# Pair sums on VectorE, a shared stationary operand for the gate weights, and a feature-major p, in a kernel of two transformer blocks

## The chip, the core and the metric

The kernel runs on one core of a Trainium2 chip. All inputs are float32 in the chip's main memory. The metric is the device time of one launch in microseconds (us), the median of several runs. TensorE is the engine for matrix products, VectorE (DVE in the profile) and ScalarE (ACT) work element by element, GpSimd (POOL) here mostly issues DMAs and adds a few tables, and SyncE (SP) issues the loads of the weights. Engines run on their own and meet only at semaphores.

## What is computed

256 tokens of width 2048 go through two blocks. Cut to what the change touches:

```
# first block, diff attention: per head (4 heads, width 256)
out = (softmax(q0 k0) - lam * softmax(q1 k1)) @ v
out = out * rsqrt(mean(out*out) + eps) * g * 0.8          # over the 256 features
# ... w_out, feed-forward ...
e = (p @ w_ple_proj) * sigmoid(rmsnorm(h) @ w_ple_gate)   # p: 256 tokens x 256
h = h + rmsnorm(e)

# second block
h = rms_norm(x)
z = h @ w_in                       # 16 of its columns are gates: mlstm input, forget, fox forget
ha = mlstm(q, k, v, gates)         # per head (4 heads, width 256)
ha = rms_norm(ha) * sigmoid(mo)    # over the head's 256 features
# ... fox attention, w_out, feed-forward ...
x = x + sigmoid(rms_norm(x) @ w_ple_gate) * (p_2 @ w_ple_proj)
```

## The kernel before

**Layout.** Activations stand feature-major: a tile is 128 features by 256 tokens, and the width of 2048 is 16 such tiles. Each float32 operand of a large product is held as two parts, hi (rounded) and lo (the rest), side by side in one array, such as `X1[:, kt, 0, :]` and `X1[:, kt, 1, :]`. A product then takes the hi part of the weights against hi and lo of the activations (512 columns, line 1923) and the lo part of the weights against hi alone (256 columns, line 1925), or three products of 512 columns (lines 1933 to 1935).

**The stream of weights.** SyncE loads weights into a ring, two halves of four tiles at a time. For each half `m` ScalarE writes the hi part (`hi`, line 589), DVE the lo part (`lo`, line 1154), and TensorE multiplies (`blocks`). ScalarE and DVE work three halves ahead (`LEAD`). Each engine's program is the same loop over halves, `each_half`: ScalarE and DVE first do the split of the half, then what `after(m)` asks for; TensorE first does what `before(m)` asks for, then the half's products. All order within an engine is this order of the program. An attention head is a group of 16 halves (`MIX`), a branch group also 16.

**The norm over a head.** A head's output of 256 features is two tiles. At the end of its group (m = 15 in diff, 13 in mLSTM, 14 in the first of them) DVE writes it to `MX[:, 0:2]`, ScalarE squares it into `MX[:, 2:4]` (`o_square`, line 690), and both go on with the next group. There, ahead of half 2, TensorE sums the squares over the features by two products with a matrix of ones (`sum_o`, lines 2058 and 2059, each float32 product appears as two records), then ScalarE takes the root (`o_norm`, line 694), DVE the reciprocal (line 1341) and the gains (line 1422 or 1730), ScalarE and DVE split the result into `X2` (lines 698 and 1346). This happens eight times, n = 0 to 7: four diff heads and four mLSTM heads. Diff head 0's sum is taken in the group of head 1, and so on; n = 3 falls into the first branch group, n = 7 into the first group of the fox attention. In the first branch group TensorE waits for `o_ready` ahead of half 4.

**The gates.** In the first mLSTM group, ahead of half 5, TensorE multiplies 16 gate columns of `w_in_2` (`gate_split`, hi and lo) by the activations: per tile one product of 512 columns (line 2223) and one of 256 (line 2224), accumulated over 16 tiles in `pw[0:16, 0]`. Then a chain of small steps counted by the semaphore `gates` follows: ScalarE copies the second half of the columns (line 955), DVE adds it (line 1664), scales and adds the bias (1666, 1668), ScalarE takes abs, exp and ln, DVE combines (1671), and TensorE turns the result ahead of half 7 (line 2231).

**p.** GpSimd loads `p` token-major into `emb[k]`. TensorE transposes it by four small products ahead of half 2 of `out1` (k = 0) and of the second `gate1` group (k = 1) (`embed`, line 2115) into `pw[:, 2]`; ScalarE writes its hi part and DVE the lo part (lines 780 and 1467) into `X2[:, 12:14]`, which the projection multiplies.

Of the kernel before, what the change touches and what calls it, by code (L numbers as in the profile page):

```python
# [170 lines left out]
def two_blocks(nc, a, out):  # L171
# [94 lines left out]
    x_turned, eps_ready, zeros_ready = sem("x_turned"), sem("eps_ready"), sem("zeros_ready")  # L266
    p_turned, p_hi, p_ready = sem("p_turned"), sem("p_hi"), sem("p_ready")
    lam_parts, lam_summed, lam_exps = (sem(n) for n in ("lam_parts", "lam_summed", "lam_exps"))
# [7 lines left out]
    probs_turned, pt_ready, pv_done = sem("probs_turned"), sem("pt_ready"), sem("pv_done")  # L276
    o_raw, o_squares, o_sums, o_root, o_normed, o_hi, o_ready = (sem(n) for n in ("o_raw", "o_squares", "o_sums", "o_root", "o_normed", "o_hi", "o_ready"))
    sig_done, gated, ple_gated, out_ready = (sem(n) for n in ("sig_done", "gated", "ple_gated", "out_ready"))
# [195 lines left out]
    def _(pool):  # L474
# [26 lines left out]
        pool.wait_ge(o_ready, 12)  # L501
        pool.dma_start(emb[0], a["p"][0, 0].rearrange("(a p) d -> p a d", p=P)).then_inc(p_landed, 16)

# [11 lines left out]
        pool.wait_ge(hid_ready, 32)  # L515
        pool.dma_start(emb[1], a["p_2"][0, 0].rearrange("(a p) d -> p a d", p=P)).then_inc(p_landed, 16)
        for j in range(6, 12):
# [56 lines left out]
    def _(act):  # L574
# [202 lines left out]
        def embed(k, operand):  # L777

            act.wait_ge(p_turned, k + 1)
            A(operand[:, :, 0, :], pw[:, 2, :].rearrange("p (a t) -> p a t", a=2), ACT.Copy).then_inc(p_hi, 1)  # L780

# [175 lines left out]
        def gate_steps(m):  # L957

            if m == 0:
                square_h(6, 0)  # L960
                square_h(6, 1)
            if m == 1:
                gained_hi(4, 3, "mix_norm_g_2")
            if m == 2:
                square_h(6, 2)
                square_h(6, 3)
            if m == 3:
                root(6)
            if m == 4:
                row(2, 3, mix_rn)  # L970
            if m == 5:

                act.wait_ge(ple_left, 16 * 4)
                gate_step(2, GR[0:16, 0], pw[0:16, 0, TOK:512], ACT.Copy)
                gate_step(5, GR[0:16, 2], GR[0:16, 1], ACT.Abs)
                gate_step(6, GR[0:16, 2], GR[0:16, 2], ACT.Exp, scale=-1.0)
                gate_step(7, GR[0:16, 2], GR[0:16, 2], ACT.Ln, bias=1.0)
            if m == 6:
                gate_step(10, small[:, 0:32], pw[:, 1, 0:32], ACT.Copy)
            if m == 7:  # L980
                gate_step(12, GR[0:16, 4], pw[0:16, 2, 0:TOK], ACT.Copy)
            if m == 9:
                gate_step(23, GR[0:4, 3], GR[0:4, 2], ACT.Exp, scale=-1.0)
                gate_step(25, small[:, 48:56], pw[:, 0, 0:8], ACT.Copy)
# [157 lines left out]
    def _(dve):  # L1142
# [191 lines left out]
        def o_lo_heads(k, tile):  # L1334
            for hh in range(2):
                dve.wait_ge(o_hi, k + hh + 1)
                TT(X2[:, bass.ds(tile + hh, 1), 1, :], pw[:, 2 + hh, 0:TOK].unsqueeze(1), X2[:, bass.ds(tile + hh, 1), 0, :], ALU.subtract).then_inc(o_ready, 1)

        def o_inverse_root(n):
            dve.wait_ge(o_root, n + 1)  # L1340
            steps.step(nc.vector.reciprocal(rn[:, 1, :], rn[:, 0, :]))
            settled()
# [37 lines left out]
        def diff(i):  # L1380
# [14 lines left out]
            def after(m):  # L1395
                if m == 3:
                    evac_normed(s, 0, QK[:, 0:2, :], mix_rn)
                if m == 7:
                    evac_normed(s, 1, QK[:, 2:4, :], mix_rn)
                    turn_by_angles(s)  # L1400
                if m == 8:
                    swap_halves()
                if m == 9:
                    rope_sum()
                if m == 11:
                    evac_values(s, 2, 0)
                if m == 12:
                    logits(2 * i + 8, 2 * i + 8, mask_tables, SCALE)
                    combine()
                if m == 15:  # L1410
                    dve.wait_ge(pv_done, 8 + i + 1)
                    nc.vector.tensor_copy(MX[:, 0:2, :], pw[:, 2:4, 0:TOK]).then_inc(o_raw, 1)
                    evac_normed(s, 3, t[:, (s.u + 3) % 2], mix_rn)
                if m == 2 and not isinstance(i, int):
                    finish_diff(i - 1)
# [12 lines left out]
        def branch(i):  # L1428
            s = At("branch", i, 8, 6)

            def after(m):
                if isinstance(i, int) and i == 0 and m == 2:
                    finish_diff(3)
# [31 lines left out]
        def embed(k, operand):  # L1465
            dve.wait_ge(p_hi, k + 1)
            TT(operand[:, :, 1, :], pw[:, 2, :].rearrange("p (a t) -> p a t", a=2), operand[:, :, 0, :], ALU.subtract).then_inc(p_ready, 1)

# [185 lines left out]
        def gate_steps(m):  # L1654
# [7 lines left out]
            if m == 5:  # L1662
                dve.wait_ge(gates, 2)
                TT(GR[0:16, 1], pw[0:16, 0, 0:TOK], GR[0:16, 0], ALU.add).then_inc(gates, 1)
                dve.wait_ge(gates, 3)
# [21 lines left out]
        def mlstm(i):  # L1687
            s = At("mlstm", i, 8, 4)
            first = isinstance(i, int)

            def after(m):
                if m == 2 and not first:
                    finish_mlstm(i - 1)
# [44 lines left out]
        def fox(i):  # L1738
# [16 lines left out]
            def after(m):  # L1755
# [14 lines left out]
                if m == 16:  # L1770
                    o_lo_heads(16 + 4 * i, 8 + 4 * i)
                if i == 0 and m == 2:
                    finish_mlstm(3)
# [128 lines left out]
    def _(pe):  # L1902
# [152 lines left out]
        def sum_o(n):  # L2055

            pe.wait_ge(o_squares, n + 1)
            MM(pw[:, 1, 0:TOK], ones, MX[:, 2, :], start=True, stop=False)
            MM(pw[:, 1, 0:TOK], ones, MX[:, 3, :], start=False, stop=True).then_inc(o_sums, 1)

# [48 lines left out]
        loop(pe, Chain(None), 4, 0, lambda i: each_half(At("branch", i, 8, 6), BRANCH), start=1)  # L2109
        def embed(k):  # L2110

            pe.wait_ge(p_landed, 16 * (k + 1))
            for f in range(2):
                for q in range(2):
                    ins = T(pw[:, 2, f * TOK + q * P:f * TOK + q * P + P], emb[k][:, q, f * P:f * P + P], ident)
            ins.then_inc(p_turned, 1)

        def out1(i):
            s = At("out1", i, 8, 2)

            def before(m):
                if i == 0 and m == 2:
                    embed(0)
            each_half(s, OUT1, x1_is(1), before)
        out1(0)
# [77 lines left out]
        each_half(at, GATE, x1_is(3), last_turn, start=4)  # L2203
        each_half(At("gate1", 1, 8, 2), GATE, x1_is(3), lambda m: embed(1) if m == 2 else None)

# [9 lines left out]
        def gate_steps(m):  # L2215
# [3 lines left out]
            if m == 5:  # L2219
                norm_row(2, 3)  # L2220
                pe.wait_ge(gate_split_lo, 1)
                for kt in range(KT):
                    MM(pw[0:16, 0, :], gate_split[:, kt, 0, :], X1[:, kt], start=kt == 0, stop=False, skip_group_check=True)
                    ins = MM(pw[0:16, 0, 0:TOK], gate_split[:, kt, 1, :], X1[:, kt, 0, :], start=False, stop=kt == KT - 1, skip_group_check=True)
                ins.then_inc(gates, 1)
# [164 lines left out]
```

## Time and profile before

| | us |
|---|---|
| median of 3 runs | 2807.81 (2807.31 to 2809.17) |
| the profiled execution, device time | 2807.58 |
| its span, first to last instruction | 2805.8 |
| TensorE busy, of the span | 2768.0 (99%) |
| DVE busy | 1801.6 (64%) |
| ScalarE busy | 1377.4 (49%) |
| mean granted clock of TensorE | 0.998 |

The profile's times count from the first instruction of the one execution that was recorded. "PE" is TensorE's products and "PEld" its weight loads, which run beneath the products. A line such as "x2" merges two neighbouring instructions. A product's record lasts longer than the distance to the next one, since products are pipelined: what a product costs is read from start to start. "Idle before" in square brackets is the time in which the engine waited, and what ended the wait.

### The profile page before, as it was taken

To read this page: it belongs to the slowest core of one execution; us is meant where nothing else is said; L and a number is where in the kernel's file an instruction comes from. 1 tells how busy PE (TensorE), PEld (TensorE's weight loads), DVE (VectorE), ACT (ScalarE), POOL (GpSimd) and SP (SyncE) were. 2 spreads that over 40 slices of the span, in tenths; PEclk is the share of its full clock that TensorE was granted. 3 is DMA by queue.
4 is the path that set the end of the run, shared out by engine and by line. 5 is a ranking of instruction groups with operands and counts; after the bars stand their busy time and mean duration, and the time that the engine had idled before them with its cause. 6 is when DMAs were issued, how large, how long until landed. Compare 5 with 4: busy or idle time off the path is not lost.

```text
span 2805.8 us, 39633 instructions
## 1 busy us (share of the span) xinstructions
PE 2768.0 (99%) x14572; PEld 2358.9 (84%) x14572; DVE 1801.6 (64%) x2112; ACT 1377.4 (49%) x1751; POOL 54.9 (2%) x67
## 2 busy tenths in 40 slices
PE   8999999999999999999999999999999999999999
PEld 6888888888888888888877888878888888888887
DVE  7676766665655656556566666775676567657655
ACT  4555554455544434444466555554544345444453
POOL 2000000000000000000000100000000000000000
PEclk9999999999999999999999999999999999999999
DMA  8555546565566565565655555545555555555654
GB/s 263 178 179 166 177 159 196 191 195 181 181 204 186 194 194 180 195 193 196 195 187 184 196 169 169 158 139 191 181 193 191 192 186 179 199 191 180 232 186 136
DMA packets 413227, 521.98 MB, mean 186 GB/s; under 512 B 8544, under 2 KB 320048, under 8 KB 412496
## 3 DMA queue, kind: packets, MB, share of 16 engines
q1 hardware_dynamic: 410384, 510.64, 55.8%
q0 software_dynamic: 2752, 10.11, 1.3%
q8 instruction: 59, 0.97, 0.1%
q14 instruction: 32, 0.26, 0.0%
HBM read 516.51 MB, written 4.21 MB: 186 GB/s over the span
## 4 chain that ended last, share of the span: by engine, by line
PE 93%; DVE 4%; ACT 2%; issue 1%; DMA 0%; SPq 0%; ACTq 0%; DVEq 0%
PE ps L1923 38%; PE ps L1925 19%; PE ps L1933 11%; PE ps L1935 11%; PE ps L1934 11%; DVE E L1744 1%; DVE split L1154 1%; PE pw L2041 1%; ACT split L589 1%; PE pw L1988 0%; DVE X L1264 0%; PE pw L2042 0%; ACT junk L628 0%; PE pw L2036 0%; DMA raw<-in_w_in 0%
## 5 line engine op out<-in xcount | busy, mean ns | idle before, releaser
L1154 DVE TENSOR_TENSOR split<-raw,split 128x1024 fp32r<-128x1024 f32 x960 | 1157.1, 1226 | 678.3 <-ACT split L589 673.4
L589 ACT ACTIVATE split<-raw 128x1024 fp32r<-128x1024 f32 x960 | 1002.8, 1055 | 823.1 <-PE ps L1935 446.4
L1923 PE MATMUL ps<-X,split 128*128 128x512 f32 x4352 | 1376.5, 398 | 12.6 <-DVE split L1154 8.5
L1925 PEld LDWEIGHTS ps<-X,split 128*128 128x128 f32 x4352 | 818.7, 188 | 193.6
L1925 PE MATMUL ps<-X,split 128*128 128x256 f32 x4352 | 856.2, 278 | 0.0
L1923 PEld LDWEIGHTS ps<-X,split 128*128 128x128 f32 x4352 | 666.1, 189 | 16.4 <-issue 10.2
L1933 PE MATMUL ps<-split,X 128*128 128x512 f32 x1408 | 550.3, 391 | 4.7 <-ACT E L805 1.2
L1935 PE MATMUL ps<-split,X 128*128 128x512 f32 x1408 | 548.1, 389 | 0.0
L1934 PE MATMUL ps<-split,X 128*128 128x512 f32 x1408 | 547.9, 389 | 0.0
L1933 PEld LDWEIGHTS ps<-split,X 128*128 128x128 f32 x1408 | 264.3, 188 | 60.8 <-DVE split L1154 1.9
L1935 PEld LDWEIGHTS ps<-split,X 128*128 128x128 f32 x1408 | 264.3, 188 | 55.0
L1934 PEld LDWEIGHTS ps<-split,X 128*128 128x128 f32 x1408 | 264.4, 188 | 54.2
L595 ACT ACTIVATE cross<-ps 128x512 f32<-128x512 f32 x160 | 95.7, 598 | 256.9 <-PE ps L1925 256.9
L1923 PE MATMUL ps<-split,X 128*128 128x512 f32 x512 | 163.0, 400 | 0.3 <-ACT small L666 0.3
L1925 PEld LDWEIGHTS ps<-split,X 128*128 128x128 f32 x512 | 96.2, 188 | 22.7
L1167 DVE TENSOR_TENSOR t<-ps,cross 128x512 f32<-128x512 f32 x74 | 51.2, 691 | 85.2 <-ACT cross L595 85.2
L1925 PE MATMUL ps<-split,X 128*128 128x256 f32 x512 | 100.6, 278 | 0.0
L1923 PEld LDWEIGHTS ps<-split,X 128*128 128x128 f32 x512 | 78.3, 189 | 2.9 <-issue 2.3
L1167 DVE TENSOR_TENSOR E<-ps,cross 128x512 f32<-128x512 f32 x54 | 37.3, 690 | 48.4 <-ACT cross L595 47.3
L845 ACT ACTIVATE X<-t 128x512 f32 (+1 forms) x32 | 20.2, 632 | 74.9 <-DVE t L1528 74.9
L1530 DVE TENSOR_TENSOR X<-t,X 128x512 f32 (+1 forms) x32 | 22.2, 692 | 32.2 <-ACT X L845 32.2
L1097 ACT ACTIVATE X<-t 128x512 f32 (+1 forms) x22 | 13.9, 631 | 52.4 <-DVE t L1845 52.4
(237 smaller groups left out, 1147.2 us busy)
## 6 DMA issues: line engine op xcount, KB each, us to landing
raw<-in_w_up SPq DMA_DIRECT2D x152, 1024.0 KB, 5.5
raw<-in_w_in SPq DMA_DIRECT2D x134, 1024.0 KB, 5.2
raw<-in_w_down SPq DMA_DIRECT2D x108, 1024.0 KB, 5.2
raw<-in_w_out SPq DMA_DIRECT2D x32, 1024.0 KB, 5.1
raw<-in_w_ple_gate SPq DMA_DIRECT2D x32, 1024.0 KB, 5.2
raw<-in_w_br_moba SPq DMA_DIRECT2D x8, 1024.0 KB, 5.5
raw<-in_w_br_diff SPq DMA_DIRECT2D x8, 1024.0 KB, 5.3
raw<-in_w_ple_proj SPq DMA_DIRECT2D x4, 1024.0 KB, 5.3
```

Source lines behind the costliest of these rows:

```text
L589: A(split[:, k % RING, :, 0, :], raw[:, (k // 2) % RING, HALF * (k % 2):HALF * (k % 2) + HALF, :], ACT.Copy).then_inc(hi_done, 1)
L595: A(cross[:, s], ps[:, 2 * s:2 * s + 2, TOK:512], ACT.Copy).then_inc(cross_done, 1)
L1154: TT(split[:, k % RING, :, 1, :], raw[:, (k // 2) % RING, HALF * (k % 2):HALF * (k % 2) + HALF, :], split[:, k % RING, :, 0, :], ALU.subtr ...
L1167: steps.step(TT(dst, ps[:, 2 * s:2 * s + 2, 0:TOK], cross[:, s], ALU.add))
L1530: TT(X2[:, bass.ds(4 * i + 2 * u, 2), 1, :], tile, X2[:, bass.ds(4 * i + 2 * u, 2), 0, :], ALU.subtract).then_inc(hid_ready, 1)
L1744: steps.step(nc.vector.reciprocal(MX, MX))
L1923: MM(ps[:, 2 * s + j, :], stay[:, 0, j * P:j * P + P], move, start=start, stop=False, skip_group_check=True)
L1925: ins = MM(ps[:, 2 * s + j, 0:TOK], stay[:, 1, j * P:j * P + P], move[:, 0, :], start=False, stop=stop, skip_group_check=True)
L1933: MM(dst, x_hi, w[:, :, 0, :], start=start, stop=False, skip_group_check=True)
L1934: MM(dst, x_hi, w[:, :, 1, :], start=False, stop=False, skip_group_check=True)
L1935: ins = MM(dst, x_lo, w[:, :, 0, :], start=False, stop=stop, skip_group_check=True)
L2041: MM(pw[:, bank, 0:TOK], values(0), pt[:, 0:TOK], start=True, stop=False, skip_group_check=True)
```

## The change

Three edits. First, DVE adds the two tiles of squares into `MX[:, 2]` (`o_pair_sum`) in `after(1)` of the group in which `sum_o` falls, and `sum_o` takes one ones-product, which waits for that addition instead of for the squares. Second, the hi and lo parts of the gate weights, 16 columns each, are one stationary operand of 32 columns: one product of 512 columns per tile, with output in 32 partitions. ScalarE copies all of it, and DVE brings partitions 16 to 31 down with a shuffle and makes two additions instead of one. Third, `p` and `p_2` are stored feature-major before the launch, so GpSimd's loads bring them as they are needed, the transposes go, and ScalarE and DVE split them straight from the loaded array. The diff, cut:

```diff
@@ gpsimd
-        pool.dma_start(emb[0], a["p"][0, 0].rearrange("(a p) d -> p a d", p=P)).then_inc(p_landed, 16)
+        pool.dma_start(emb[0], a["p_t"].rearrange("p (f t) -> p f t", f=2)).then_inc(p_landed, 16)
...
-        pool.dma_start(emb[1], a["p_2"][0, 0].rearrange("(a p) d -> p a d", p=P)).then_inc(p_landed, 16)
+        pool.dma_start(emb[1], a["p_2_t"].rearrange("p (f t) -> p f t", f=2)).then_inc(p_landed, 16)
@@ scalar
         def embed(k, operand):
-            act.wait_ge(p_turned, k + 1)
-            A(operand[:, :, 0, :], pw[:, 2, :].rearrange("p (a t) -> p a t", a=2), ACT.Copy).then_inc(p_hi, 1)
+            act.wait_ge(p_landed, 16 * (k + 1))
+            A(operand[:, :, 0, :], emb[k], ACT.Copy).then_inc(p_hi, 1)
...
-                gate_step(2, GR[0:16, 0], pw[0:16, 0, TOK:512], ACT.Copy)
+                gate_step(2, GR[0:32, 0:2], pw[0:32, 0, :].rearrange("p (a t) -> p a t", a=2), ACT.Copy)
@@ vector
+        def o_pair_sum(n):
+            dve.wait_ge(o_squares, n + 1)
+            TT(MX[:, 2, :], MX[:, 2, :], MX[:, 3, :], ALU.add).then_inc(o_pair_sums, 1)
...
         def diff(i), after(m)
+                if m == 1 and not isinstance(i, int):
+                    o_pair_sum(i - 1)
                 if m == 2 and not isinstance(i, int):
                     finish_diff(i - 1)
...
         def branch(i), after(m)
+                if isinstance(i, int) and i == 0 and m == 1:
+                    o_pair_sum(3)
...
         def embed(k, operand):
             dve.wait_ge(p_hi, k + 1)
-            TT(operand[:, :, 1, :], pw[:, 2, :].rearrange("p (a t) -> p a t", a=2), operand[:, :, 0, :], ALU.subtract).then_inc(p_ready, 1)
+            TT(operand[:, :, 1, :], emb[k], operand[:, :, 0, :], ALU.subtract).then_inc(p_ready, 1)
...
                 dve.wait_ge(gates, 2)
-                TT(GR[0:16, 1], pw[0:16, 0, 0:TOK], GR[0:16, 0], ALU.add).then_inc(gates, 1)
+                steps.step(nc.vector.stream_shuffle(GR[0:32, 2], GR[0:32, 0], HALVES_SWAPPED))
+                steps.step(TT(GR[0:16, 1], GR[0:16, 0], GR[0:16, 1], ALU.add))
+                settled()
+                TT(GR[0:16, 1], GR[0:16, 1], GR[0:16, 2], ALU.add).then_inc(gates, 1)
...
         def mlstm(i), after(m)
+                if m == 1 and not first:
+                    o_pair_sum(i + 3)
...
         def fox(i), after(m)
+                if i == 0 and m == 1:
+                    o_pair_sum(7)
@@ tensor
         def sum_o(n):
-            pe.wait_ge(o_squares, n + 1)
-            MM(pw[:, 1, 0:TOK], ones, MX[:, 2, :], start=True, stop=False)
-            MM(pw[:, 1, 0:TOK], ones, MX[:, 3, :], start=False, stop=True).then_inc(o_sums, 1)
+            pe.wait_ge(o_pair_sums, n + 1)
+            MM(pw[:, 1, 0:TOK], ones, MX[:, 2, :], start=True, stop=True).then_inc(o_sums, 1)
...
-        def embed(k):
-            pe.wait_ge(p_landed, 16 * (k + 1))
-            for f in range(2):
-                for q in range(2):
-                    ins = T(pw[:, 2, f * TOK + q * P:f * TOK + q * P + P], emb[k][:, q, f * P:f * P + P], ident)
-            ins.then_inc(p_turned, 1)
...
                 for kt in range(KT):
-                    MM(pw[0:16, 0, :], gate_split[:, kt, 0, :], X1[:, kt], start=kt == 0, stop=False, skip_group_check=True)
-                    ins = MM(pw[0:16, 0, 0:TOK], gate_split[:, kt, 1, :], X1[:, kt, 0, :], start=False, stop=kt == KT - 1, skip_group_check=True)
+                    ins = MM(pw[0:32, 0, :], gate_split[:, kt].rearrange("p a c -> p (a c)"), X1[:, kt], start=kt == 0, stop=kt == KT - 1)
                 ins.then_inc(gates, 1)
@@ host
+    for name in ("p", "p_2"):
+        arrays[name + "_t"] = np.ascontiguousarray(arrays.pop(name)[0, 0].T.reshape(2, P, TOK).transpose(1, 0, 2)).reshape(P, 2 * TOK)
```

## Rows read from the trace of the kernel before

**Rows 1.** The page, busy time, share of the span and instructions of each engine.
```profile
PE 2768.0 (99%) x14572; PEld 2358.9 (84%) x14572; DVE 1801.6 (64%) x2112; ACT 1377.4 (49%) x1751; POOL 54.9 (2%) x67
```

**Rows 2.** TensorE's waits, whole run: who for whom, total us, times, longest.
```profile
PE ps L1923 <- DVE split L1154: 8.5, 3, 7.9
PE pw L2029 <- DVE E L1747: 4.0, 2, 2.0
...
PE pw L2036 <- DVE E L1393: 1.9, 4, 0.5
```

**Rows 3.** Order of time, 260 to 276: start, us, instruction, [idle before].
```profile
268.28 2.36 DVE L1154 TENSOR_TENSOR split<-raw,split 128x1024 fp32r<-128x1024 f32 x2 [1.99 <-ACT split L589]
...
269.61 0.59 PE L2058 MATMUL pw<-E,con 128*128 128x256 f32 x2
...
270.04 0.59 PE L2059 MATMUL pw<-E,con 128*128 128x256 f32 x2
```

**Rows 4.** Order of time after the second diff head, 311 to 324, and 320.9.
```profile
318.46 3.50 DVE L1154 TENSOR_TENSOR split<-raw,split 128x1024 fp32r<-128x1024 f32 x3 [3.05 <-ACT split L589]
...
318.73 0.59 PE L2058 MATMUL pw<-E,con 128*128 128x256 f32 x2
...
320.74 1.22 DVE L1154 TENSOR_TENSOR split<-raw,split 128x1024 fp32r<-128x1024 f32 x1
```

**Rows 5.** Order of time at the last diff head and the branch after it.
```profile
416.67 3.50 DVE L1154 TENSOR_TENSOR split<-raw,split 128x1024 fp32r<-128x1024 f32 x3 [3.04 <-ACT split L589]
...
416.96 0.59 PE L2058 MATMUL pw<-E,con 128*128 128x256 f32 x2
...
419.85 0.48 ACT L694 ACTIVATE rn<-pw,small 128x256 f32<-128x256 f32 x1
...
423.72 0.69 DVE L1346 TENSOR_TENSOR X<-E,X 128x512 fp32r<-128x512 f32 x1 [0.70 <-ACT X L698]
...
424.47 0.73 PE L1923 MATMUL ps<-X,split 128*128 128x512 f32 x2 [0.91 <-DVE X L1346]
```

**Rows 6.** Order of time after the second mLSTM head, 1627 to 1632.
```profile
1627.92 2.36 DVE L1154 TENSOR_TENSOR split<-raw,split 128x1024 fp32r<-128x1024 f32 x2 [1.65 <-ACT split L589]
...
1629.60 0.59 PE L2058 MATMUL pw<-E,con 128*128 128x256 f32 x2
```

**Rows 7.** Groups by line and shape: total us, mean ns, idle before.
```profile
L1306 DVE STREAM_SHUFFLE E<-E 32x1024 f32<-32x1024 f32 x8 | 10.7, 1343 | 0.0
...
L1717 DVE TENSOR_TENSOR rn<-rn,G 128x256 f32<-128x256 f32 x4 | 1.7, 420 | 1.1 <-ACT rn L1004 1.1
...
L780 ACT ACTIVATE X<-pw 128x512 fp32r<-128x512 f32 x2 | 1.1, 571 | 0.0
```

**Rows 8.** Order of time around the gate weights' matmuls, 1530 to 1548.
```profile
1537.68 0.39 PE L2223 MATMUL pw<-X,gate_split 128*16 128x512 f32 x1
...
1537.91 0.28 PE L2224 MATMUL pw<-X,gate_split 128*16 128x256 f32 x1
...
1538.02 0.63 PE L1923 MATMUL ps<-X,split 128*128 128x512 f32 x2
...
1538.28 0.37 ACT L955 ACTIVATE E<-pw 16x256 f32<-16x256 f32 x1 [4.28 <-PE pw L2224]
...
1543.36 0.40 PE L1925 MATMUL ps<-X,split 128*128 128x256 f32 x2
...
1544.43 0.26 PE L2231 MATMUL pw<-con,E 16*128 16x16 f32 x2 [0.67 <-DVE E L1671]
```

**Rows 9.** Order of time around the first `embed`, 588 to 602.
```profile
597.01 0.39 PE L1935 MATMUL ps<-split,X 128*128 128x512 f32 x1
...
597.91 0.40 PE L1934 MATMUL ps<-split,X 128*128 128x512 f32 x1
```

**Rows 10.** Stretches: length, busy us of each engine, granted clock, DMA share, GB/s.
```profile
24.00:28.00 4.00, 4.00 (x14) 3.41 (x13) 4.00 (x9) 0.04 (x1) 0.00 (x0) 0.50 0.68 236
...
1881.00:1891.00 10.00, 7.99 (x41) 6.76 (x41) 9.04 (x25) 5.75 (x13) 0.00 (x0) 1.00 0.31 106
```

More of the change, by code:

```diff
@@ L266, in two_blocks @@
     x_turned, eps_ready, zeros_ready = sem("x_turned"), sem("eps_ready"), sem("zeros_ready")
-    p_turned, p_hi, p_ready = sem("p_turned"), sem("p_hi"), sem("p_ready")
+    p_hi, p_ready = sem("p_hi"), sem("p_ready")
     lam_parts, lam_summed, lam_exps = (sem(n) for n in ("lam_parts", "lam_summed", "lam_exps"))
@@ L276, in two_blocks @@
     probs_turned, pt_ready, pv_done = sem("probs_turned"), sem("pt_ready"), sem("pv_done")
-    o_raw, o_squares, o_sums, o_root, o_normed, o_hi, o_ready = (sem(n) for n in ("o_raw", "o_squares", "o_sums", "o_root", "o_normed", "o_hi", "o_ready"))
+    o_raw, o_squares, o_pair_sums, o_sums, o_root, o_normed, o_hi, o_ready = (sem(n) for n in ("o_raw", "o_squares", "o_pair_sums", "o_sums", "o_root", "o_normed", "o_hi", "o_ready"))
     sig_done, gated, ple_gated, out_ready = (sem(n) for n in ("sig_done", "gated", "ple_gated", "out_ready"))
@@ L2109, in _ @@
         loop(pe, Chain(None), 4, 0, lambda i: each_half(At("branch", i, 8, 6), BRANCH), start=1)
-        def embed(k):
-            pe.wait_ge(p_landed, 16 * (k + 1))
-            for f in range(2):
-                for q in range(2):
-                    ins = T(pw[:, 2, f * TOK + q * P:f * TOK + q * P + P], emb[k][:, q, f * P:f * P + P], ident)
-            ins.then_inc(p_turned, 1)
-        def out1(i):
[L2119 to L2124, printed above, removed]
+        def out1(i):
+            each_half(At("out1", i, 8, 2), OUT1, x1_is(1))
         out1(0)
@@ L2203, in _ @@
         each_half(at, GATE, x1_is(3), last_turn, start=4)
-        each_half(At("gate1", 1, 8, 2), GATE, x1_is(3), lambda m: embed(1) if m == 2 else None)
+        each_half(At("gate1", 1, 8, 2), GATE, x1_is(3))
         s = At("proj2")
```

## The prediction

> **What bounds the kernel now.** I read the page first: TensorE is busy for 99% of the span [rows 1]. That share alone is modelled, so the second view is what TensorE waited for [rows 2]. The list adds up to 31 us in 2805.8, of which 7.9 is one wait at the start. In the body TensorE runs from matmul to matmul, and the other engines work in its shadow. So whatever is taken off TensorE is gained, and whatever it is made to wait for is lost, almost one for one. The third view is the order of time around each place that the diff touches. There I look for two things: where TensorE stands when it reaches the changed instruction, and where VectorE (DVE) stands at that moment.
>
> **Pair sums: what TensorE saves.** A ones-product of 256 fp32 columns takes 0.43 us: the first starts at 269.61 and the second at 270.04 [rows 3]. Eight calls lose one each: 8 x 0.43 = 3.4 us less.
>
> **Pair sums: the new wait.** TensorE now waits, ahead of half 2 of the next unit group, for an addition that DVE issues in `after(1)`, so behind `lo(0)` and `lo(1)` of that group. Before, it waited for ScalarE's squares, which were long there. The question is where DVE is at that time. It is late: ScalarE squares, waits and takes the sigmoid at the end of the group before, and only then turns to the next halves' splits, so DVE's run of subtractions begins after 3.05 us of idleness, at 318.46. TensorE is at the ones-products at 318.73, when `lo(0)` has hardly begun [rows 4]. The third subtraction of that run starts at 320.74, which is 2.28 us after the first. Nothing holds it back there, so the pair sum takes this very place. Queued behind it on DVE is the third subtraction (half 5's operand), which TensorE needs over 8 us later (a half takes about 2.8 us), so the delay there costs nothing.
> An addition of 128x256 fp32 takes 0.42 us [rows 7]. From DVE's end to TensorE's start I take 0.06 us (423.72 + 0.69 = 424.41, then 424.47) [rows 5]. With S for the start of DVE's first subtraction, the product starts at S + 2.28 + 0.42 + 0.06 = S + 2.76. It takes 0.43, and I add 0.10 for a first matmul after an idle time, an estimate from row 424.47, where two matmuls show 0.73 and not the usual 0.63 [rows 5, 8]. So half 2 begins at S + 3.29. Before it began at T + 0.86 (two products), T being the start of the first. The loss is (S - T) + 2.43.
> - n = 0: S = 268.28, T = 269.61 [rows 3]: 1.10 us. ScalarE loads its table early in this unrolled stretch, so S is earlier.
> - n = 1: 318.46 and 318.73 [rows 4]: 2.16. n = 2 repeats it (S - T = -0.28): 2.15. n = 4, the first mLSTM head's, is the same picture with -0.22: 2.21.
> - n = 5: 1627.92 and 1629.60 [rows 6]: 0.75. n = 6 and 7 repeat it to 0.01: 2.25 for the three.
> - n = 3: 416.67 and 416.96 give 2.14. But here TensorE already lost 1.06 us two halves later, waiting for `o_ready`: it started at 424.47 after 0.91 by the row [rows 5]. Such idle times come out some 0.15 short, since a matmul's record runs past the start of the next (0.67 and 0.83 in rows 8, below), so it was free at 423.41. Now it comes there at 416.67 + 3.29 + 5.6 = 425.56. The chain before `o_ready` starts with a square root at 419.85, whose table is loaded already. The new product ends about 420.2, so the chain moves by 0.35 us, to 424.8, and the wait is gone. The loss at n = 3 is 425.56 - 424.57 = 0.99. If the table load should come behind the wait, it would be 1.6.
> Sum: 1.10 + 2.16 + 2.15 + 0.99 + 2.21 + 2.25 = 10.9 us lost, the saved products already deducted. What follows `sum_o` (square root, reciprocal, gains) starts no later relative to TensorE than before, since TensorE itself was held, so I find no second stall. The handover may be 0.15 instead of 0.06 and the first matmul's 0.10 may be nothing: 10.1 to 11.7, and up to 12.3 with n = 3.
>
> **Gate weights.** Before, each of 16 tiles has a matmul of 512 and one of 256 columns, starting 0.23 and 0.11 to 0.12 us apart [rows 8]. Sixteen times 0.115 is 1.8 us less. The weight loads, 32 instead of 16 columns, lie beneath the 512-column matmuls, as the 128-column loads do elsewhere; if they did not, the gain would shrink towards 0. But the chain behind it grows. TensorE already waits at the end of it: 0.67 by the row, but the last two matmuls start at 1543.36 and 1543.48, so TensorE was free at 1543.60 and the wait to 1544.43 is 0.83 us [rows 8]. ScalarE's copy goes from 16x256 (0.37) to 32x512, taken as 0.57 from the 128x512 copy out of the same PSUM tensor [rows 7, 8]: +0.20. DVE does a shuffle and one more addition. The 32x1024 shuffle takes 1.34 us [rows 7], a subtraction of 1024 columns 1.22 [rows 4] and an addition of 256 columns 0.42 [rows 7], so I estimate 0.55 for a 256-column shuffle (between 0.34, a quarter, and 0.55, the same fixed share) and 0.42 for the addition, less overlap: +0.93. The wait grows by 1.13 us, and the part nets 1.13 - 1.84 = -0.7. Bounds: -1.8 (nothing of the chain exposed) to +0.2 (a slower shuffle, a smaller gain).
>
> **p comes feature-major.** The four transposes of `embed` take 0.44 us: matmuls of 512 columns start 0.23 us apart [rows 8], and between the starts at 597.01 and 597.91, two such steps, 0.90 pass [rows 9]. Twice: -0.88 us. ScalarE's copy and DVE's subtraction read SBUF instead of PSUM at 512 columns, where rows differ by under 0.1 us, and TensorE waits for neither. The DMAs stay on the GpSimd queue at the same points, with the same bytes, and land long before use. Bounds 0 to -1.0.
>
> **Sum.** 10.9 - 0.7 - 0.9 = +9.3 us on the profiled execution's 2807.58 us (span 2805.8, so 1.8 around it): 2816.9. The median of the runs shown, 2807.81, is 0.2 higher; I say 2817.0, +0.33%.
>
> **Rivals.**
> *The pair sums are hidden (the other side).* If DVE has its two subtractions done before TensorE gets there, so S before T - 2.8, no stall is left: -3.4 - 0.7 - 0.9 = -5.0, so 2802.8. The part pays as long as the mean stall is under 0.43. For it: TensorE reaches the product two full halves into the group, and DVE needs only two subtractions by then. Against it: at none of the eight places is S earlier than T - 1.7 [rows 3, 4, 6]. 7%.
> *The stalls are given back.* TensorE waits for its late helpers elsewhere, 1.9 us in front of the probabilities' transposes [rows 2]. If its delay let them catch up there and at one or two such places: about 2814.5. Against it: these waits hang on TensorE's own scores one or two halves earlier. 8%.
> *The clock falls.* After the 7.9 us wait at the start [rows 2], TensorE had 0.50 of the clock, 1.2 GHz, from 24 to 28 us; around the 2.0 us wait for line 1747 [rows 2] it kept 1.00, 2.4 GHz [rows 10]. The four longest new stalls, 2.5 us, lie between, nearer to the second. Four microseconds at half clock are 2 us lost; after four stalls +8, so 2825. 5%. [...]
>
> **How the numbers follow.** Forecast 80%, the three rivals 7, 8 and 5%. The forecast's own bounds are 10.1 to 12.3, -1.8 to +0.2 and -1.0 to 0: 2814.9 to 2820.1 at the extremes. The range 2812.0 to 2821.5 adds the giving back and some room for a stall misjudged by half a microsecond at several places; the first and third rivals are left out. About 0.2%, 5.6 us, is what a measurement of this kernel can tell from no change, so the borders are 2802.2 and 2813.4. Faster: 0.05 (the first rival lies just inside its border, so most of it, should more than I see be hidden). Same: 0.14 (the rest of it, some of the giving back, stalls 0.5 us shorter than I think). Slower: 0.81.
>
> **What the new profile would show.** TensorE's waits should have a row for `sum_o`'s product behind DVE's new addition: eight times, some 1.4, 2.5, 2.5, 2.5, 2.5 and three of 1.1 us, 15 in total. The wait of line 1923 for line 1346 should be gone. One product per call, 16 gate matmuls, no transposes in `embed`. The wait ahead of the transposed gate rows should be about 2 us. The granted clock should stay 1.00 there. I am wrong if DVE's addition starts before the second subtraction, or if the stalls are there and the time is not.

## The result, and the profile after

| | before | changed |
|---|---|---|
| median, same chip | 2808.65 us (2807.31 to 2809.17) | 2820.19 us (2819.14 to 2823.07) |
| ratio | 1 | 1.0043 (1.0033 to 1.0054) |
| the profiled execution, device time | 2807.58 | 2821.43 |
| its span | 2805.8 | 2819.6 |
| mean granted clock of TensorE | 0.998 | 0.996 |

The change costs 11.5 us in the median. The direction is as forecast, and 2820.19 lies in the range (2812.0 to 2821.5), 3.2 us above the 2817.0. Between the two profiled executions it is 13.85 us, against a sum of 9.3. So there are two questions: are the stalls what they were worked out to be, and what are the other 2 to 4.5 us?

Lines of the changed kernel have moved: the ones-product of `sum_o` is L2073, the new addition L1341, the products of the stream L1938 and L1940 (1923 and 1925 before), the gate product L2224. First the page's row of busy times, the answer to [rows 1]:

```profile
PE 2766.8 (98%) x14532; PEld 2357.5 (84%) x14532; DVE 1805.5 (64%) x2123; ACT 1378.6 (49%) x1751; POOL 54.2 (2%) x67
```

TensorE has 40 product records fewer and is busy 1.2 us less (its slow stretches count as busy too), while the span is 13.8 us longer: the time went into waiting. TensorE's waits of the changed kernel, the answer to [rows 2] (who for whom, total us, times, longest):

```profile
PE pw L2073 <- DVE E L1341: 13.6, 8, 2.7
PE ps L1938 <- DVE split L1154: 9.8, 3, 9.3
PE pw L2044 <- DVE E L1760: 4.0, 2, 2.0
...
PE pw L2231 <- DVE E L1682: 1.7, 1, 1.7
```

The first row is new: the ones-product waits for the pair sum eight times, 13.6 us. The last row is the gate chain's wait, 0.67 before [rows 8] and now 1.7. The wait of the stream for line 1346, 0.91 at n = 3 [rows 5], is gone from the list. Next the order of time around n = 1, the answer to [rows 4] (start, us, instruction, idle before):

```profile
316.92 2.94 ACT L589 ACTIVATE split<-raw 128x1024 fp32r<-128x1024 f32 x3
...
318.00 2.36 DVE L1154 TENSOR_TENSOR split<-raw,split 128x1024 fp32r<-128x1024 f32 x2 [3.05 <-ACT split L589]
...
320.27 0.42 DVE L1341 TENSOR_TENSOR E<-E 128x256 f32<-128x256 f32 x1
320.61 1.22 DVE L1154 TENSOR_TENSOR split<-raw,split 128x1024 fp32r<-128x1024 f32 x1
...
320.75 0.70 PE L2073 MATMUL pw<-E,con 128*128 128x256 f32 x2 [2.32 <-DVE E L1341]
...
321.98 1.03 PE L1938 MATMUL ps<-X,split 128*128 128x512 f32 x2
```

DVE was idle for 3.05 us, then did the first two subtractions of its order (`lo(0)` and `lo(1)`), and only then, 2.27 us after the first of them began, the addition; TensorE stood still until 0.06 us after its end (320.27 + 0.42, then 320.75). The last row is what the forecast did not hold: two products of the stream take 1.03 us where they take 0.63 at full clock. The granted clock over the same stretch (window, its length, busy time of PE, PEld, DVE, ACT and POOL, granted clock, DMA share, GB/s):

```profile
320.00:322.00 2.00, 1.25 (x7) 1.12 (x8) 1.83 (x4) 1.63 (x2) 0.00 (x0) 1.00 0.64 182
322.00:324.00 2.00, 2.00 (x8) 1.70 (x7) 1.97 (x2) 0.00 (x0) 0.00 (x0) 0.50 1.09 377
324.00:326.00 2.00, 2.00 (x9) 1.67 (x8) 0.94 (x3) 0.81 (x2) 0.00 (x0) 0.65 1.10 350
326.00:328.00 2.00, 2.00 (x14) 1.74 (x13) 1.50 (x2) 0.88 (x1) 0.00 (x0) 1.00 0.44 140
```

After the 2.32 us of standing still the clock falls from 1.00 to 0.50 (1.2 GHz), and 8 products are done in two microseconds instead of 14.

**Where the 13.85 us lie.** The total is the same instruction's start in two traces, subtracted. I took ScalarE's 160 evacuations of a product's result (line 595 in both kernels) as landmarks: between two of them the difference changes only where something was lost or won. The steps, in us (worked out from the starts in the order of time of both traces):

| place | changed, profiled | forecast | what the rest is |
|---|---|---|---|
| after the wait at the start | -1.54 | 0 | the clock came back sooner after it; chance |
| n = 0 | +1.09 | +1.10 | |
| n = 1 | +3.70 | +2.16 | clock 0.50, then 0.65 |
| n = 2 | +3.58 | +2.15 | clock 0.50, then 0.85 |
| n = 3 | +0.97 | +0.99 | |
| `p`, twice | -0.47, -0.46 | -0.44 each | |
| gates | +0.70 | -0.7 | clock 0.50 |
| n = 4 | +4.15 | +2.21 | clock 0.50, then 0.71; 0.37 ahead of it, not explained |
| n = 5, 6, 7 | +0.75, +0.75, +0.76 | +0.75 each | |
| all else | 0 | 0 | |

The places without a clock fall are met to 0.03 us. Four places have one, and there the loss is some 1.4 to 1.6 us above the working (at n = 4 after the 0.37 is taken off). The start is not the same from one execution to the next: by the same landmarks it lies between -1.55 and +1.37 us of the kernel before's over the twelve other traces.

### The profile page after: what moved, and what is told of

The parts are those of the page before. It is cut to its first block, busy times and chain, and to the rows that moved or that the text cites. A ratio compares the mean times of both kernels' runs of the same rounds, so it can differ in the third digit from the quotient of the medians.

```text
span 2819.6 us, 39564 instructions
## 1 busy us (share of the span) xinstructions
PE 2766.8 (98%) x14532; PEld 2357.5 (84%) x14532; DVE 1805.5 (64%) x2123; ACT 1378.6 (49%) x1751; POOL 54.2 (2%) x67
## 4 chain that ended last, share of the span: by engine, by line
PE 91%; DVE 5%; ACT 2%; issue 1%; DMA 0%; ACTq 0%; DVEq 0%; SPq 0%
PE ps L1938 37%; PE ps L1940 18%; PE ps L1948 11%; PE ps L1950 11%; PE ps L1949 11%; DVE split L1154 1%; DVE E L1757 1%; ACT split L589 1%; PE pw L2056 1%; PE pw L2003 0%; DVE X L1264 0%; PE pw L2057 0%; ACT junk L628 0%; PE pw L2051 0%; ACT cross L595 0%
## 5 line engine op out<-in xcount | busy, mean ns | idle before, releaser
L1938 PE MATMUL ps<-X,split 128*128 128x512 f32 x4352 | 1379.8, 398 | 13.1 <-DVE split L1154 9.8
L1940 PEld LDWEIGHTS ps<-X,split 128*128 128x128 f32 x4352 | 820.7, 189 | 194.4
L1940 PE MATMUL ps<-X,split 128*128 128x256 f32 x4352 | 857.7, 278 | 0.0
L1938 PEld LDWEIGHTS ps<-X,split 128*128 128x128 f32 x4352 | 667.9, 189 | 16.9 <-issue 11.5
L1938 PE MATMUL ps<-split,X 128*128 128x512 f32 x512 | 163.0, 400 | 0.3 <-ACT small L666 0.3
L1940 PEld LDWEIGHTS ps<-split,X 128*128 128x128 f32 x512 | 96.2, 188 | 22.7
L1940 PE MATMUL ps<-split,X 128*128 128x256 f32 x512 | 100.6, 278 | 0.0
L1938 PEld LDWEIGHTS ps<-split,X 128*128 128x128 f32 x512 | 78.3, 189 | 2.9 <-issue 2.3
```

Source lines behind the costliest of these rows:

```text
L1938: MM(ps[:, 2 * s + j, :], stay[:, 0, j * P:j * P + P], move, start=start, stop=False, skip_group_check=True)
L1940: ins = MM(ps[:, 2 * s + j, 0:TOK], stay[:, 1, j * P:j * P + P], move[:, 0, :], start=False, stop=stop, skip_group_check=True)
```

## The experiments

Their names and medians, each with the kernel before on the same chip:

| run | kernel | median us (range) | before | ratio (interval) |
|---|---|---|---|---|
| e1 | pair sums alone | 2820.59 (2819.18 to 2823.42) | 2808.44 | 1.0043 (1.0029 to 1.0057) |
| e2 | gate edit alone | 2806.50 (2805.61 to 2810.14) | 2808.44 | 0.9995 (0.9986 to 1.0004) |
| e3 | p alone | 2808.03 (2805.45 to 2810.34) | 2808.44 | 0.9999 (0.9990 to 1.0008) |
| e4 | the wait alone | 2821.58 (2820.79 to 2822.02) | 2808.44 | 1.0046 (1.0032 to 1.0059) |
| e5 | pair sum one half earlier | 2809.64 (2808.28 to 2813.64) | 2808.47 | 1.0005 (0.9996 to 1.0014) |
| e6 | pair sum in its own group | 2805.81 (2804.49 to 2807.07) | 2808.47 | 0.9989 (0.9980 to 0.9998) |
| e7 | e6 without the gate edit | 2805.04 (2802.93 to 2805.83) | 2808.47 | 0.9988 (0.9979 to 0.9997) |
| e8 | waits at n = 0 to 3 filled | 2820.78 (2819.04 to 2824.83) | 2808.47 | 1.0047 (1.0033 to 1.0061) |
| e9 | changed, once more | 2820.67 (2820.39 to 2822.96) | 2808.69 | 1.0044 (1.0031 to 1.0058) |
| e10 | the long new waits filled | 2816.23 (2815.79 to 2819.99) | 2808.69 | 1.0028 (1.0017 to 1.0038) |
| e11 | e6, gate wait filled | 2802.39 (2801.65 to 2806.43) | 2808.69 | 0.9981 (0.9972 to 0.9990) |

**e1, the pair sums alone.** `p` and the gates are as before; what is left of the change:

```diff
+        def o_pair_sum(n):
+            dve.wait_ge(o_squares, n + 1)
+            TT(MX[:, 2, :], MX[:, 2, :], MX[:, 3, :], ALU.add).then_inc(o_pair_sums, 1)
...
-            MM(pw[:, 1, 0:TOK], ones, MX[:, 2, :], start=True, stop=False)
-            MM(pw[:, 1, 0:TOK], ones, MX[:, 3, :], start=False, stop=True).then_inc(o_sums, 1)
+            MM(pw[:, 1, 0:TOK], ones, MX[:, 2, :], start=True, stop=True).then_inc(o_sums, 1)
```

> The kernel before with the pair sums alone, put where the change puts them (after DVE's second subtraction of the next group); gate weights and p stay as they were. Theory: this part alone makes the kernel slower. In the trace of the changed kernel the eight places account for 1.09, 3.69, 3.58, 0.97, 4.15, 0.75, 0.76 and 0.73 us, so some 15.7 with the clock falls after the three longest stalls (about 1.5 each) and 10.9 without them: plus 11 to 16 us on the median. Rival: the slowdown is spread over all three edits, then this one gives under 8 us.

It costs 12.2 us in the median. By landmarks n = 0, 1, 2 and 3 cost 1.10, 2.16, 2.16 and 0.97 us, n = 5 to 7 0.75, 0.74 and 0.74. With no clock fall in these seven places, all of them lie on the working, n = 1 and 2 too, where the changed kernel's own trace had 3.70 and 3.58. n = 4 costs 3.76, with a fall. Two more falls sit at TensorE's waits for the pair that [rows 2] shows as line 2029 behind line 1747, 2.0 us long, which this edit does not touch: the clock was 0.50 after both, where the kernel before had 1.00 around them ([rows 10] shows the second). These two cost 1.64 and 1.59 us. So this execution has three falls, and only one of them is where the changed kernel's had its four.

**e2, the gate edit alone, and e3, p alone.**

```diff
@@ e2, tensor
-                    MM(pw[0:16, 0, :], gate_split[:, kt, 0, :], X1[:, kt], start=kt == 0, stop=False, skip_group_check=True)
-                    ins = MM(pw[0:16, 0, 0:TOK], gate_split[:, kt, 1, :], X1[:, kt, 0, :], start=False, stop=kt == KT - 1, skip_group_check=True)
+                    ins = MM(pw[0:32, 0, :], gate_split[:, kt].rearrange("p a c -> p (a c)"), X1[:, kt], start=kt == 0, stop=kt == KT - 1)
...
@@ e3, scalar, vector (TensorE's embed is gone)
-            A(operand[:, :, 0, :], pw[:, 2, :].rearrange("p (a t) -> p a t", a=2), ACT.Copy).then_inc(p_hi, 1)
+            A(operand[:, :, 0, :], emb[k], ACT.Copy).then_inc(p_hi, 1)
```

> The kernel before with the shared stationary operand of the gate weights alone. Theory: TensorE saves 1.84 us and waits 0.98 us longer for the longer chain, so minus 0.9 us where the clock holds, and plus 0.7 where it falls to 1.2 GHz after that wait, as in the profiled execution of the changed kernel. Rival: the wait costs nothing new, minus 1.8 us.

> The kernel before with p and p_2 stored feature-major alone. Theory: two sets of transposes go, 0.47 and 0.50 us, so minus 1.0 us. Rival: the DMAs of the new layout or the reads from SBUF cost something, then zero or plus.

Neither is told from no change by its median; the landmarks are finer. The gate edit alone gains 0.86 us, with no fall after its wait. `p` alone gains 0.52 and 0.50. The medians of the three parts add up to 12.2 - 1.9 - 0.4 = 9.8 us for the whole change's 11.5, within what their intervals leave open.

**e4, is it the wait or the addition?** Both products stay and nothing is added on DVE; TensorE merely waits for DVE's second subtraction of the group (`lo(1)`), behind which the addition would stand:

```diff
+            pe.wait_ge(lo_done, at.halves(1 + LEAD) + 1)
             pe.wait_ge(o_squares, n + 1)
             MM(pw[:, 1, 0:TOK], ones, MX[:, 2, :], start=True, stop=False)
             MM(pw[:, 1, 0:TOK], ones, MX[:, 3, :], start=False, stop=True).then_inc(o_sums, 1)
```

> The kernel before, with nothing added but a wait: ahead of each pair of ones-products TensorE waits for DVE's second subtraction of the group (the one that the pair sum stands behind). No addition, and both products stay. Theory: the place in DVE's order is what costs, not the addition. The product can start at S + 2.37 + 0.06, against S + 2.76 with the addition, and costs 0.43 more, so the sum of the losses is about the same, plus 11 us without clock falls, and up to plus 16 with them. Rival: the addition itself or its semaphore is what costs; then this kernel is within 3 us of the kernel before.

The wait by itself costs what the whole part costs: 1.21, 2.27, 2.25 and 1.05 at n = 0 to 3, 3.97 at n = 4 (with a fall), 0.92, 0.92 and 0.84 behind. The addition's own 0.42 us and the saved product's 0.43 cancel, so each place stands 0.1 to 0.2 us from e1. TensorE's waits of e4:

```profile
PE pw L2059 <- DVE split L1154: 10.8, 8, 2.1
```

So it is the place in DVE's order, not the addition's price.

**e5, one half earlier.** The addition moves from `after(1)` to `after(0)` in all four loops:

```diff
-                if m == 1 and not isinstance(i, int):
+                if m == 0 and not isinstance(i, int):
                     o_pair_sum(i - 1)
```

> The changed kernel with the pair sum one place earlier in DVE's order, behind the first subtraction of the group and ahead of the second. Theory: the sum is ready 1.14 us earlier, so the stalls fall from 1.3, 2.5, 2.5, 2.5, 2.7 and three of 1.1 us to 0.2, 1.3, 1.3, 1.3, 1.5 and three of nearly nothing; the losses shrink by about 8 us, and by up to 4.5 more if the shorter stalls leave the clock at 2.4 GHz: about plus 1 us against the kernel before. Rival: the second subtraction, now 0.4 us later, starves TensorE instead, then the gain is under 5 us.

One subtraction ahead of it instead of two. TensorE's waits, and the order of time at n = 4:

```profile
PE pw L2073 <- DVE E L1341: 5.1, 4, 1.6
...
1581.87 1.23 DVE L1154 TENSOR_TENSOR split<-raw,split 128x1024 fp32r<-128x1024 f32 x1 [1.65 <-ACT split L589]
1583.01 0.42 DVE L1341 TENSOR_TENSOR E<-E 128x256 f32<-128x256 f32 x1
...
1583.49 0.70 PE L2073 MATMUL pw<-E,con 128*128 128x256 f32 x2 [1.60 <-DVE E L1341]
```

13.6 us of waiting became 5.1. Where the stall was longer than one subtraction it is shorter by one: n = 1, 2 and 4 cost 0.97, 0.96 and 1.01 where they cost 2.16, 2.16 and 2.21 without a clock fall, and n = 0, 3 and 5 to 7 cost nothing or gain up to 0.40. No place lost the clock. The kernel is 1.2 us above before where the changed one is 11.5 above.

**e6, in its own group.** DVE's addition moves to half 15 of the head's own group, behind what DVE does there anyway and ahead of its idle time:

```diff
                 if m == 15:
+                    o_pair_sum(i)
...
-                if m == 1 and not isinstance(i, int):
-                    o_pair_sum(i - 1)
```

> The changed kernel with the pair sum at the end of the head's own group on DVE, behind the last scaling, when ScalarE's squares are done. Theory: no stall is left at all, and each of the eight places saves its product: minus 3.4, minus 1.0 for p, minus 0.9 (or plus 0.7 with a clock fall) for the gates: 2803.3 to 2805. Rival: DVE's addition there delays the subtractions behind it and starves TensorE at the start of the next group; then it is not faster than the kernel before.

Now the part does what it says. At n = 1 the addition runs at 315.02, the product goes through at 318.43 with no idle before it, and DVE's three subtractions follow one another:

```profile
315.02 0.42 DVE L1341 TENSOR_TENSOR E<-E 128x256 f32<-128x256 f32 x1
...
318.16 3.50 DVE L1154 TENSOR_TENSOR split<-raw,split 128x1024 fp32r<-128x1024 f32 x3 [2.71 <-ACT split L589]
318.20 0.39 PE L1934 MATMUL ps<-X,split 128*128 128x256 f32 x2
318.43 0.59 PE L2067 MATMUL pw<-E,con 128*128 128x256 f32 x2
```

Seven of the eight places gain 0.44 us, one product. n = 3 gains nothing: there the saved product only brings TensorE sooner to its wait for `o_ready`, 0.91 us before [rows 5] and 1.35 here:

```profile
423.31 0.73 PE L1932 MATMUL ps<-X,split 128*128 128x512 f32 x2 [1.35 <-DVE X L1350]
```

The kernel is 2.7 us faster than before in the median. Without a clock fall the parts would give 7 x 0.44 + 0.6 for `p` + 0.86 = 4.5; in the profiled execution the gate wait's fall (+0.71 where e2 had -0.86) and one at the 2.0 us wait at 1798 (+1.63) take 3.2 of them. The median is 0.8 us above the expected 2803.3 to 2805.

The 0.6 for `p` is 0.10 at the first place and 0.48 at the second, where e3 has 0.52 and 0.50. At the first one most of the saved time turns into another wait: two products of the stream, which start 0.23 us apart elsewhere, start 0.50 apart there (598.56 and 599.06).

**e7, e6 with the gates as before.**

```diff
-                    ins = MM(pw[0:32, 0, :], gate_split[:, kt].rearrange("p a c -> p (a c)"), X1[:, kt], start=kt == 0, stop=kt == KT - 1)
+                    MM(pw[0:16, 0, :], gate_split[:, kt, 0, :], X1[:, kt], start=kt == 0, stop=False, skip_group_check=True)
+                    ins = MM(pw[0:16, 0, 0:TOK], gate_split[:, kt, 1, :], X1[:, kt, 0, :], start=False, stop=kt == KT - 1, skip_group_check=True)
```

> As the kernel before this one (pair sums at the end of the group, p feature-major), but with the gate weights as in the kernel before. Theory: minus 3.4 and minus 1.0, 4.4 us under the kernel before, or 2804.2. The difference from the kernel with the gate edit shows that edit once more: it should be 0.9 slower where the clock holds, and up to 0.7 faster where it falls.

2805.04 against e6's 2805.81 (2802.93 to 2805.83 and 2804.49 to 2807.07): the gate edit, worth 0.86 where its wait keeps the clock, brings nothing that the medians show. In e6's trace the wait that it lengthens lost the clock; here that wait is as short as before and kept it.

**e8, filling some waits.** If the extra 2 to 4 us are the clock, work in the waits should win them back. Ahead of the wait at n = 0 to 3 TensorE does three products of constants into an unused bank of `pw`, whose result nobody reads:

```diff
+            if filled:
+                pe.wait_ge(o_raw, n + 1)
+                for _ in range(3):
+                    MM(pw[:, 3, 0:TOK], ones, tri, start=True, stop=True)
             pe.wait_ge(o_pair_sums, n + 1)
```

> The changed kernel, with three products of 256 columns (ones against the constant table, into an unused bank) put ahead of TensorE's wait in the four diff places: 1.28 us of useless work in stalls of 1.3, 2.5, 2.5 and 2.5 us. It changes nothing that is waited for. Theory that the clock adds to the stalls: the idle part shrinks to 0 to 1.2 us, the clock holds there, and the kernel is about 3 us faster than the changed one (the two falls after n = 1 and 2), at the same stalls. Rival: the excess of 1.5 us over the stall is something else, then it is as slow as the changed kernel or slower.

The median, 2820.78, is that of the changed kernel. The kernel should have been 3 us faster by the theory and was not; the rival had it as slow. The trace is less clear: n = 1 and 2 cost 2.15 and 2.13, with the clock at 1.00, but the unfilled n = 4 (3.76) and the gates (+0.70) lost it. The run filled only some of the waits, and e1 had shown that others lose the clock too, so it could not tell the theories apart. It is inconclusive; e10 is the run that it should have been.

**e9 and e10, the changed kernel again and the long new waits filled,** on one chip (n = 7, a wait of 0.9 us, stays as it is): three useless products at n = 0 to 2, five at n = 3, two at n = 4 to 6, and three in the gate chain's wait.

```diff
+            if filled:
+                pe.wait_ge(o_raw, n + 1)
+                for _ in range(filled):
+                    MM(pw[:, 3, 0:TOK], ones, tri, start=True, stop=True)
             pe.wait_ge(o_pair_sums, n + 1)
...
-                    sum_o(i - 1)
+                    sum_o(i - 1, 3)
...
+                for _ in range(3):
+                    MM(pw[:, 3, 0:TOK], ones, tri, start=True, stop=True)
```

> The changed kernel, unaltered, beside the two kernels after it, to see in a second trace which waits the clock falls behind. Theory: the waits are the same to 0.1 us in every execution, while which of them are followed by 1.2 GHz differs; none at or under 1.6 us of recorded wait, some or most of those from 1.66 to 2.7. Rival: the falls are fixed to places, then n = 1, n = 2, n = 4 and the gate chain show them again and n = 3 does not. The median again near 2820 us.

> The changed kernel with useless products of 0.43 us each ahead of every long wait: three at n = 0, 1 and 2, five at n = 3, two at n = 4, 5 and 6, three at the gate chain. No wait ends later than before, except that n = 3 has 2.13 us of them in a 2.5 us stall. Theory: the idle parts shrink to 1.0 us and less, at n = 4 to 1.9, so at most n = 4 can lose the clock, and the kernel is faster than the changed one by the falls that it no longer has, 1.5 us each: 1.5 to 4 us. Rival: the falls happen too seldom to be seen in a median, then it is within 1 us of the changed kernel.

2820.67 and 2816.23: more work on the engine that bounds the kernel makes it 4.4 us faster, and the ranges do not touch (2820.39 to 2822.96, 2815.79 to 2819.99). In e9's trace n = 1, 2, 4 and the gates lost the clock, the same four as in the first profile of the changed kernel, and cost 3.71, 3.63, 3.76 and 0.69. That is what e9's rival said, falls fixed to places, and not its theory, that another trace would show others. Two traces can't tell a fixed pattern from chance. That executions of one kernel differ is shown by the mean granted clock that every execution has on record: of the changed kernel's eleven (with e9) four have 0.995 or 0.996 and took 2821.4 to 2823.1 us, seven have 0.997 and took 2819.1 to 2820.7. In e10's trace none of the four places lost it: 2.16, 2.16, 2.22 and -0.92, at n = 4 behind an idle time of 1.87 us that was left. Here is the granted clock after the waits of n = 1 and n = 4, first e9, then e10:

```profile
324.00:326.00 2.00, 2.00 (x8) 1.71 (x7) 1.97 (x3) 0.00 (x0) 0.00 (x0) 0.50 1.09 371
...
1595.00:1597.00 2.00, 2.00 (x9) 1.71 (x8) 1.70 (x4) 0.00 (x0) 0.00 (x0) 0.54 1.09 364
```

```profile
324.00:326.00 2.00, 2.00 (x13) 1.74 (x13) 1.97 (x3) 0.00 (x0) 0.00 (x0) 1.00 1.09 373
...
1590.00:1592.00 2.00, 2.00 (x14) 1.73 (x13) 1.82 (x3) 0.00 (x0) 0.00 (x0) 1.00 1.09 367
1810.00:1812.00 2.00, 2.00 (x7) 1.75 (x8) 2.00 (x3) 0.00 (x0) 0.00 (x0) 0.50 0.03 9
```

The last row stands behind the 2.0 us wait that was left unfilled: there e10's profiled execution did lose the clock, twice (1.62 and 1.60 us), and that execution, 2819.99 us, is 3.8 us above e10's median. Its mean granted clock is 0.997; the seven others have 0.998, which none of the changed kernel's reached.

**e11, the version that the runs point to:** e6 with three useless products in the gate chain's wait.

```diff
                 if m == 15:
+                    o_pair_sum(i)
...
+                for _ in range(3):
+                    MM(pw[:, 3, 0:TOK], ones, tri, start=True, stop=True)
```

> Pair sums at the end of the head's own group, p feature-major, the gate edit, and three useless products in the gate chain's wait, so that its idle part falls from 1.66 to some 0.4 us. Theory: the eight places give minus 3.0 (n = 3 gives nothing, its wait for the normed outputs takes it back), p minus 0.7 to 1.0, the gates minus 0.9 without a clock fall: 4.6 under the kernel before, about 2804. Against the same kernel with unfilled gate wait it should be up to 1.5 faster. Rival: the gate edit brings nothing either way, then it equals that kernel, 2805.8.

2802.39 us, 0.9981 (0.9972 to 0.9990) of the kernel before: 6.3 us faster than it, and 18.3 faster than the changed kernel on the same chip (e9). By landmarks the gates gain 0.92, `p` 0.14 and 0.49, and seven of the eight places 0.43 to 0.45 (n = 3 nothing), 4.6 us in all, with no clock fall. Its waits no longer have a row for the ones-product, and the gate chain's is 0.3 us. Against e6, on another chip, the filler is worth 3.4 us in the median, more than the 1.6 of the one fall that it covers and more than the up to 1.5 expected. The mean granted clock is 0.997 or less in all eleven of e6's executions and 0.998 in eight of e11's, so the clock is in the difference; how much of it, and whether the gate wait alone is behind it, is not shown.

## Why the prediction was right, and where it was off

That 2820.19 lies within the range is in part luck. The range's upper end of 2821.5 was room for misjudged stalls. No stall was misjudged by more than 0.05 us, but for 0.37 us ahead of n = 4, and what used the room was the clock, which the forecast had taken as steady.

**TensorE bounds the kernel, almost one for one.** Right. Outside the places named, the distance between the two traces stays the same to 0.03 us.

**The stalls of the pair sums.** Right to 0.05 us at each place, wherever the clock stayed: e1 has 1.10, 2.16, 2.16, 0.97, 0.75, 0.74, 0.74 for a working of 1.10, 2.16, 2.15, 0.99 and three of 0.75, and e10 has 2.22 for the 2.21 of n = 4. The addition took the very slot that the third subtraction had, as [rows 4] let one read. e4 shows that the wait alone is the price, e5 that each subtraction ahead of it is 1.2 us of it, e6 that without one the part gains. The waits' row that was forecast, eight times and 15 us, came as eight times and 13.6: the rows are some 0.15 us shorter than the real stall, as the prediction itself had noted of such rows.

**n = 3 loses less because a later wait goes.** Right: 0.97 for 0.99, the wait for line 1346 of [rows 5] is gone, and e6 shows the other side of it, a place where the saved product is only waited for.

**The gate products and their chain.** The products are right: 16 in 3.89 us. The chain was priced at 1.13 us more and is 0.98. The term that was too big is the shuffle, 0.43 us where 0.55 was taken between 0.34 and 0.55:

```profile
1543.26 0.59 ACT L955 ACTIVATE E<-pw 32x512 f32<-32x512 f32 x1 [2.43 <-PE pw L2224]
1543.88 0.43 DVE L1672 STREAM_SHUFFLE E<-E 32x256 f32<-32x256 f32 x1
1544.22 0.40 DVE L1673 TENSOR_TENSOR E<-E 16x256 f32<-16x256 f32 x1
...
1549.83 0.41 DVE L1682 SCALAR_TENSOR_TENSOR E<-E 16x256 f32<-16x256 f32 x1 [3.94 <-ACT E L955]
1550.39 0.26 PE L2231 MATMUL pw<-con,E 16*128 16x16 f32 x2 [1.67 <-DVE E L1682]
1550.58 1.07 PE L1938 MATMUL ps<-X,split 128*128 128x512 f32 x2
```

The net is -0.86 for -0.7, and the wait is 1.67 by its row for the forecast's "about 2". These rows, which answer to [rows 8], also hold what the part lost again: the last one shows two products at 1.07 us, half clock, after a wait of 1.67.

**p.** -0.52 and -0.50 alone, -0.47 and -0.46 within the change, for -0.44 each. That it is gained in full hangs on what comes behind it: e6, e7 and e11 have 0.10 to 0.17 at the first place.

**The clock.** This step failed, and it is nearly the whole of the distance. The forecast said that the granted clock would stay 1.00 after stalls of 2.5 us, because it did after the 2.0 us wait of [rows 10], and gave the other case 5%. That row was one execution of something that varies: in e1, e4, e6 and e10 one or both of the kernel's two waits of this kind lost the clock. What the profiled executions show of the clock in TensorE's waits and the 2.5 us after them (the idle time by its row, the clock by windows):

| wait | by its row, us | lost the clock |
|---|---|---|
| any, all runs | up to 1.60 | never |
| at the start of the kernel, one or two a run | 3.0 to 9.4 | each time, in all 13 |
| gate chain | 1.66 to 1.67 | in changed, e6, e8, e9; not in e2, e5 |
| for line 1747 (1760 changed), twice a run | 2.0 | both in e1 and e10, one in e4 and e6; in the nine others none |
| n = 1, 2, 3 in e4 | 2.0 | none |
| n = 1, 2 | 2.3 | in changed and e9 both; in e1 neither |
| n = 3 | 2.3 | never (changed, e1, e9) |
| n = 4, unfilled | 2.1 to 2.7 | in changed, e1, e4, e8, e9, each time |
| n = 4 in e10, behind two useless products | 1.9 | not |

Each fall cost 1.4 to 1.6 us, not the 2 of the rival. The rival spoke of four falls in the longest stalls and 8 us; the profiled executions of the changed kernel, e1, e4 and e8 to e10 have two to four, also at the 1.7 us gate wait that it did not name. The changed kernel's profiled execution had four, 6.1 us, and 1.5 us back at the start. e10 makes the clock the shown cause: with TensorE held up as long and with more work it is at 2816.2, and its trace has no fall at any place that the change touches; 2817.0 was the working without a fall. Against that the changed kernel's median holds some 3 to 4 us of clock. The difference to before is smaller than this, 11.5 against a sum of 9.3, because the median of before, 2808.65, is itself 1.1 above the profiled execution on which the sum was made. This 1.1 goes with the clock. Of the 66 executions of the kernel before beside e1 to e11, on three chips, those with a mean granted clock of 0.998, as the profiled one has, have medians of 2807.5 to 2807.8 us, those with 0.997 have 2808.5 to 2808.9. At which waits the clock was lost in them no trace shows; its own two 2.0 us waits are likely, by e1, e4, e6 and e10.

The Trainium skill, "TensorE: Matmul & The Clock Gate", section "Why this matters for your kernels", warns against idle gaps between bursts of products. The waits at the start, 3.0 to 9.4 us, agree with it. But the gaps that it warns of are longer than the new stalls, so read as it stands it would have let them pass, and 1.66 to 2.7 us lost the clock in these traces; the measurement decides.

**The rivals.** Hidden pair sums: none of the eight was hidden; it would have taken e6's place of the addition. Stalls given back: the landmarks show nothing given back but n = 3's, which was in the sum.

**What stays open.** What decides in which execution a wait of 1.66 to 2.3 us loses the clock, and why n = 4 unfilled always did and n = 3 never. Also 0.37 us ahead of n = 4, which appear in the changed kernel, e5, e8, e9 and e10, and not in e1, e2, e6 or e11, so with the pair sum in the next group and the gate edit together: DVE's idle ahead of line 1730 (1717 before) is 1.4 us in that group for 1.05, which I did not follow further.

## What to carry to other kernels

An operation that moves off the bounding engine onto an in-order helper costs what stands ahead of it there: read both engines in the order of time at the place, and issue it where the helper is ahead (here in the group that makes its data), not where the consumer stands. Price an added wait by its length and, here from 1.66 us on, by the clock too, and do not take the clock from one execution's row. Where such a wait can't be moved away, useless products in it can be worth more than they cost.

## What was not expected of the hardware

- TensorE's granted clock fell to 0.50 after waits as short as 1.66 us, in some traces and not in others with a wait as long, and 1.4 to 1.6 us were lost each time. No wait up to 1.60 us lost it.
- With three useless products (1.46 us by their rows) in a wait it stayed at 1.00 (n = 1 and 2 and the gate chain in e10, the gate chain in e11), and the kernel with 23 such products was 4.4 us faster.
- A shuffle of 32x256 took 0.43 us on DVE, as long as an addition of 128x256 (0.42).
